# The second block's down projection by pairs of column chunks, with 14 of its 44 block pairs as seven products

## The reference

```python
def conv_ffn(h, w_up, conv_w, conv_b, w_down):
    u = h @ w_up
    u_pad = jnp.pad(u, ((0, 0), (CONV_WIDTH_2 - 1, 0), (0, 0)))
    u = sum(conv_w[j] * u_pad[:, j:j + s] for j in range(CONV_WIDTH_2)) + conv_b
    gate, up = jnp.split(u, 2, axis=-1)
    return (jax.nn.silu(gate) * up) @ w_down
...
        ff = conv_ffn(rms_norm(h, g_ffn_pre[i]), w_up[i], conv_w[i], conv_b[i], w_down[i])
        h = h + rms_norm(ff, g_ffn_post[i])
        e = p[i] @ w_ple_proj[i]
        gate = jax.nn.sigmoid(rms_norm(h, g_ple_in[i]) @ w_ple_gate[i])
        h = h + rms_norm(e * gate, g_ple_post[i])
```

## Time and profile before

| | us |
|---|---|
| median of three runs | 2400.28 (2399.91 to 2403.27) |
| the profiled execution | 2402.21 |
| its span in the trace | 2400.4 |
| PE busy | 2389.7 |
| DVE busy | 1730.3 |
| ACT busy | 1351.6 |
| PE's share of the chain that ended last | 98% |
| granted clock of TensorE, mean | 0.999 |

### The profile page before, as it was taken

How to read it: one execution, slowest core, us unless ns; L and a number is a source line. 1 busy time by engine, 2 the same in 40 slices (tenths; PEclk the granted TensorE clock), 3 DMA queues, 4 the chain that set the end, 5 groups by cost and what they waited for, 6 DMA issues and landing times.

```text
span 2400.4 us, 36297 instructions
## 1 busy us (share of the span) xinstructions
PE 2389.7 (100%) x13245; PEld 2019.9 (84%) x13245; DVE 1730.3 (72%) x2181; ACT 1351.6 (56%) x1729; POOL 47.3 (2%) x105
## 2 busy tenths in 40 slices
PE   9999999999999999999999999999999999999999
PEld 7888888888888888888888888898888888888887
DVE  6578765888888889797578575577777777644475
ACT  5467754555555566456655455466566566444464
POOL 3300000000000000000000000000000000000000
PEclk9999999999999999999999999999999999999999
DMA  8643546566666666656665556566565665666664
GB/s 266 193 143 114 156 160 185 178 206 195 203 188 204 192 198 207 208 190 196 180 186 171 155 154 193 175 201 193 185 196 188 185 194 184 214 194 193 211 197 146
DMA packets 235104, 448.57 MB, mean 187 GB/s; under 512 B 14368, under 2 KB 31604, under 8 KB 234480
## 3 DMA queue, kind: packets, MB, share of 16 engines
q1 hardware_dynamic: 231712, 434.83, 58.0%
q0 software_dynamic: 3280, 12.21, 1.7%
HBM read 443.84 MB, written 3.15 MB: 186 GB/s over the span
## 4 chain that ended last, share of the span: by engine, by line
PE 98%; ACT 1%; DVE 1%; DMA 0%; issue 0%; SPq 0%; ACTq 0%; DVEq 0%
PE pg L2923 12%; PE pg L2925 12%; PE pg L2924 12%; PE pg L3406 7%; PE pg L3408 7%; PE pg L3407 7%; PE pt L3578 7%; PE pg L3578 6%; PE pg L3582 3%; PE pt L3582 3%; PE pg L2982 3%; PE pg L2983 3%; PE pg L2984 3%; PE pt L3408 2%; PE pt L3406 2%; PE pt L3407 2%
## 5 line engine op out<-in xcount | busy, mean ns | idle before, releaser
L1735 DVE TENSOR_TENSOR wlo<-raw,whi 128x1024 fp32r<-128x1024 f32 (+3 forms) x755 | 890.8, 1192 | 545.5 <-ACT whi L826 542.9
L826 ACT ACTIVATE whi<-raw 128x1024 fp32r<-128x1024 f32 (+3 forms) x799 | 819.8, 1034 | 777.4 <-PE pg L2925 412.6
L3578 PE MATMUL pt<-A,whi 128*128 128x512 f32 x704 | 244.8, 391 | 0.0
L3578 PE MATMUL pg<-A,whi 128*128 128x512 f32 x640 | 222.3, 391 | 0.0
L2923 PE MATMUL pg<-whi,A 128*128 128x512 f32 (+1 forms) x576 | 221.5, 385 | 0.0
L2925 PE MATMUL pg<-whi,A 128*128 128x512 f32 (+1 forms) x576 | 218.0, 378 | 0.0
L2924 PE MATMUL pg<-wlo,A 128*128 128x512 f32 (+1 forms) x576 | 217.8, 378 | 0.0
L3582 PE MATMUL pg<-A,wlo 128*128 128x256 f32 x704 | 197.3, 280 | 0.0
L3582 PE MATMUL pt<-A,wlo 128*128 128x256 f32 x704 | 197.1, 280 | 0.0
L3578 PEld LDWEIGHTS pt<-A,whi 128*128 128x128 f32 x704 | 131.7, 187 | 28.9
L3578 PEld LDWEIGHTS pg<-A,whi 128*128 128x128 f32 x640 | 119.7, 187 | 26.2
(11 more groups left out here) (667 smaller groups left out, 4675.9 us busy)
## 6 DMA issues: line engine op xcount, KB each, us to landing
raw<-w_up SPq DMA_DIRECT2D x264, 512.0 KB, 4.4
raw<-w_down SPq DMA_DIRECT2D x176, 512.0 KB, 4.6
raw<-w_in SPq DMA_DIRECT2D x151, 512.0 KB, 3.8
raw<-w_gate SPq DMA_DIRECT2D x88, 512.0 KB, 3.7
raw<-w_out SPq DMA_DIRECT2D x64, 512.0 KB, 3.8
raw<-w_ple_gate SPq DMA_DIRECT2D x32, 512.0 KB, 4.6
raw<-w_in SPq DMA_DIRECT2D x32, 388.0 KB, 3.3
raw<-w_in SPq DMA_DIRECT2D x16, 280.0 KB, 3.0
```

The costliest lines, as they stand in the source:

```text
L826: A(whi[:, n % RING, 0:w], raw[:, n % RING, 0:w], ACT.Copy).then_inc(hi_ready, 1)
L1735: V.tensor_tensor(wlo[:, n % RING, 0:w], raw[:, n % RING, 0:w], whi[:, n % RING, 0:w].bitcast(F32), ALU.subtract).then_inc(lo_ready, 1)
L3578: mm(o.rearrange("p (a n) -> p a n", a=2), wh, A2[:, :, kt, :], start=first, stop=False)
```

## The change

`D_SEVEN` gets a second entry, for the second block: six blocks of the first half (5, 9, 11, 13, 15, 18) and eight of the second (4, 6, 8, 10, 12, 14, 16, 18) are taken as seven products. The loads come in pairs of chunks. The product of the convolution goes to FR in fp32, and FH and FL are made from it in groups of four tiles: group 0 in the second pair of the feed forward loop, the other ten inside the first half of the down projection (`f_hi_part`, `f_lo_part`). ACT does the last pair's convolution ahead of block 6, DVE ahead of block 7. The sums of the activations have only two homes here, so all eight of the second half are made. The results go to FOD by way of sums on DVE; ACT squares them there, and DVE multiplies with the gain (`f_gained`) inside the second half. `last_steps` isn't used in this projection any more. The gain is loaded once the last product of the convolution is there.

```diff
-D_SEVEN = (((3, 6, 8, 12, 14, 18), (3, 6, 8, 10, 12, 14, 16, 18)),)
+D_SEVEN = (((3, 6, 8, 12, 14, 18), (3, 6, 8, 10, 12, 14, 16, 18)), ((5, 9, 11, 13, 15, 18), (4, 6, 8, 10, 12, 14, 16, 18)))
...
-                elif name in ("down1",):
+                elif name in ("down1", "down2"):
...
-                pool.wait_ge(f_lo, 2 * NFF)
+                pool.wait_ge(c_prod, NFF)
                 load(GP[:], a["g_ffn_post_2"][0].partition_broadcast(P), gain_landed)
-                pool.wait_ge(step_used, G["down2"]["N"] + 3 * G["down2"]["S"] + 8)
+                pool.wait_ge(step_used, d_step(1, 1, 7, 0))
...
                 pair(0, 0, between)
-                with act.Fori(0, NFF - 1) as i:
-                    pair(1, i)
+                pair(1, 0, {8: lambda: f_hi_part(1, 0)})
+                with act.Fori(0, NFF - 2) as i:
+                    pair(2, i)
...
-            def f2_hi(c, d):
-                act.wait_ge(c_prod, c + d)
-                A(FH[:, ds((d + c - 1) * 4, 4), :], UC[:], ACT.Copy).then_inc(f_hi, 1)
...
+            def f_squares(p, t, m):
+
+                act.wait_ge(chunk_out[t], DN[1]["C"] + 2 * p + m + 1)
+                act.wait_ge(c_prod, NFF)
+                if p or m:
+                    act.wait_ge(sq_ready, 8 + 4 * p + 2 * m)
+                A(JD[:, t, :], FOD[p][:, t, m * CW:(m + 1) * CW], ACT.Square, accum_out=PS[:, t, 2 * p + m:2 * p + m + 1]).then_inc(sq_ready, 1)
+
+            def down2():
+
+                for p in range(2):
+                    for q in range(2, DQ):
+                        if p == 0 and q == 2:
+                            f2_up(NFF, 0)
+                            d_group(1, 1)
+                        if p == 0 and q == 6:
+                            f2_conv_up(NFF, 0)
+                        if p == 1 and q == 3:
+                            p_parts(1, PHD)
+                        d_blocks(1, p, q)
+                        if p == 0 and q % 2 and q < DQ - 1:
+                            d_group(1, (q + 1) // 2)
+                        if q == D_SEVEN[1][p][-1] + 1:
+                            d_first(1, p)
+                    if p == 0:
+                        for q in range(2):
+                            d_blocks(1, 1, q)
+                            for t in range(NT):
+                                f_squares(0, t, q) if q == 0 else f_squares(0, 1 - t, q)
+                split(DN[1]["end"])
+                split(DN[1]["end"] + 1)
+                root_table()
+                f_squares(1, 0, 0)
+                f_squares(1, 1, 0)
+                f_squares(1, 1, 1)
+                f_squares(1, 0, 1)
...
-                V.tensor_tensor(UC[:], UC[:], GC[:], ALU.mult).then_inc(c_prod, 1)
+                V.tensor_tensor(FR[:, ds((d + c - 1) * 4, 4), :], UC[:], GC[:], ALU.mult).then_inc(c_prod, 1)
...
+                for p in range(2):
+                    y0, y1, y2 = Y0[1][p][:], Y1[1][p][:], Y2[1][p][:]
+                    for q in range(2, DQ - 2):
+                        if p == 0 and q == 2:
+                            f2_up(NFF, 0)
+                            f_lo_part(1, 1)
+                        if p == 0 and q == 7:
+                            f2_conv_up(NFF, 0)
+                        if p == 1 and q == 3:
+                            p_parts(1, PHD, PLD)
+                        if p == 1 and q == 5:
+                            f_gained(0, 0, 0, 1)
+                            f_gained(0, 1, 0, 2)
+                        if p == 1 and q == 7:
+                            f_gained(0, 1, 1, 3)
+                            f_gained(0, 0, 1, 4)
+                        d_blocks(1, p, q)
+                    dve.wait_ge(t_used, d_done(1, p))
+                    add(p, 2, y1, b["P6"], y0)
+                    if p == 0:
+                        d_group(1, DQ // 2 - 1)
...
+                    n = d_step(1, p, DQ, 0)
+                    split(n)
+                    dve.wait_ge(p_run, d_run(1, p, 1))
+                    last(p, 0, 0, b["P2"], y0)
+                    split(n + 1)
+                    dve.wait_ge(step_used, n - 1)
+                    last(p, 1, 0, b["P4"], y2)
+                    if p:
+                        f_gained(1, 0, 0, 1)
+                    else:
+                        split(n + 2)
+                    dve.wait_ge(p_run, d_run(1, p, 2))
+                    last(p, 1, 1, b["X22"], out(1, p, 1))
+                    if p:
+                        f_gained(1, 1, 0, 2)
+                    dve.wait_ge(step_used, n)
+                    last(p, 0, 1, b["P3"], y1)
+                    if p == 0:
+                        split(n + 3)
...
-            down(G["down2"], no, NFF, turn_p)
+            for p in range(2):
+                for q in range(DQ):
+                    if p and q == 2:
+                        pe.wait_ge(u_sum, d_sum(1, 0, 3))
                         p_turn()
+                    d_blocks(1, p, q)
```

More of the change, by code:

```diff
@@ L1618, in _ @@
             if upto < 17: return
-            ffn(F2, [after(f2_up), after(f2_conv_up), lambda c, d: (f2_gate(c, d), after(f2_hi)(c, d)), after(f2_conv_gate)],
+            ffn(F2, [after(f2_up), after(f2_conv_up), f2_gate, after(f2_conv_gate)],
                 {2: f2_in(2), 4: f2_in(3), 6: norm_ffn2, 12: f2_roots, 14: lambda: f2_conv_gate(0, 0)})
[L1622 to L1632, removed]
+            def f_squares(p, t, m):
[4 more added lines that the diff above has]
+                A(JD[:, t, :], FOD[p][:, t, m * CW:(m + 1) * CW], ACT.Square, accum_out=PS[:, t, 2 * p + m:2 * p + m + 1]).then_inc(sq_ready, 1)
@@ L1633, in _ @@
+            down2()
             take_root(7, D)
@@ L1659, in gate_out @@
                 if c == 3 and t == 0:
-                    act.wait_ge(half_used, 3)
+                    act.wait_ge(half_used, 2)
                 else:
@@ L2200, in ffn @@
                 pair(0, 0, between)
-                with dve.Fori(0, NFF - 1) as i:
-                    pair(1, i)
+                pair(1, 0, {9: lambda: f_lo_part(1, 0)})
+                with dve.Fori(0, NFF - 2) as i:
+                    pair(2, i)
             def down(g, hooks, evac, between={}):
@@ L2798, in last_add @@
                 f2_in(2)()
-            ffn(F2, [after(f2_up), after(f2_conv_up), after(lambda c, d: (f2_gate(c, d), f2_lo(c, d))), after(f2_conv_gate)],
+            ffn(F2, [after(f2_up), after(f2_conv_up), after(f2_gate), after(f2_conv_gate)],
                 {1: last_add, 4: f2_in(3), 7: lambda: rstd(6, D), 13: f2_gate_first, 15: lambda: f2_conv_gate(0, 0)})
[L2803 to L2811, removed]
+            def f_gained(p, t, m, n):
+                if p == 0 and n == 1:
+                    dve.wait_ge(gain_landed, 48)
+                dve.wait_ge(sq_ready, 8 + 4 * p + n)
+                x = FOD[p][:, t, m * CW:(m + 1) * CW]
+                ins = V.tensor_tensor(x, x, GP[:, (2 * p + m) * CW:(2 * p + m + 1) * CW], ALU.mult)
+                if n % 2 == 0:
+                    ins.then_inc(gained, 1)
@@ new lines, in down2, with add, last @@
+            def down2():
+                b = d_banks[1]
+                out = lambda t, p, m: FOD[p][:, t, m * CW:(m + 1) * CW]
+                def add(p, i, o, x, y):
+                    dve.wait_ge(u_sum, d_sum(1, p, i - 1))
+                    V.tensor_tensor(o, x, y, ALU.add).then_inc(u_sum, 1)
+                def last(p, t, m, bank, y):
+                    dve.wait_ge(u_sum, d_sum(1, p, 5))
+                    V.tensor_tensor(out(t, p, m), bank, y, ALU.add).then_inc(chunk_out[t], 1)
+                for p in range(2):
[19 more added lines that the diff above has]
+                        d_group(1, DQ // 2 - 1)
+                    split(d_step(1, p, DQ - 2, 0))
+                    add(p, 3, y2, b["P7"], y1)
+                    split(d_step(1, p, DQ - 2, 1))
+                    add(p, 4, y1, b["P5"], y1)
+                    split(d_step(1, p, DQ - 1, 0))
+                    add(p, 5, out(1, p, 1), b["P5"], y2)
+                    split(d_step(1, p, DQ - 1, 1))
+                    n = d_step(1, p, DQ, 0)
[17 more added lines that the diff above has]
+                        split(n + 3)
@@ L2828, in _ @@
             split(g["N"] + 3)
-            post_add(FO, 2)
+            dve.wait_ge(gained, 7)
+            post_add(FOD[1], 2, 2)
             def last_add():
-                evac(3, 0, G["down2"]["end"])
+                f_gained(1, 1, 1, 3)
+                f_gained(1, 0, 1, 4)
                 ple_in(2)()
                 dve.wait_ge(gained, 8)
-                post_add(FO, 3)
+                post_add(FOD[1], 3, 2)
             between = {(0, 1): last_add, (0, 4): ple_in(3), (0, 7): lambda: rstd(8, D)}
@@ L3952, in _ @@
             chunks_read(pe, g["C"] - 1)
-            proj(2, PH, PL)
-            proj(3, PH, PL, lambda: part_0(6, 2))
+            proj(2, PHD, PLD)
+            proj(3, PHD, PLD, lambda: part_0(6, 2))
             pe.wait_ge(h_block, 5)
```

24 lines of the change are left out of this document (9 added, 15 removed).

## The result

The changed kernel takes 2408.22 us (median of 10, 2407.85 to 2410.58); the kernel before took 2401.07 us in 10 runs (2399.83 to 2403.27). The ratio is 1.0030, with a 95% interval of 1.0021 to 1.0038: slower by 7.15 us, where 9.4 was forecast. Fourteen blocks of the second down projection do with 42 matmuls less, and TensorE waits longer than that saves.

What follows compares the result with a forecast made beforehand. PE was taken as the bound, with DVE too slow to feed it: -9.52 + 1.03 + 6.8 + 0.5 + 9.0 + 0.6 + 1.0 = +9.4 us, giving 2409.7 us; own range 2404 to 2415, whole range 2398 to 2420.

Steps and rivals of the forecast that it cites:

- The start: Start of the second block's down projection: PE waits for bank half X22 until DVE's addition ends; +1.03 us.
- How DVE and PE keep step: Down projection: PE waits at a seven-product block if DVE began it under 4.37 us earlier; second-half pairs 11.13 against 10.20.
- Second half: Down projection's second half, blocks 4 to 18: DVE needs 80.3 us, PE 71.4, so PE waits; +9.0 us.
- The lead at block 4: Second half: distance from DVE's start of block 4 to PE's start of it, 4.4 us, nothing to spare.
- First half: Down projection's first half: waits of 0.2 twice, then DVE's pairs 2.12 us short three times; +6.8 us, bounds 4 and 8.
- the gain's load: First half, about T + 37: the moved load may delay the load block 9 waits for; +0.5 us.
- Restarts: Matmuls behind some 12 waits in both halves, recorded with 0.47 instead of 0.39; +1.0 us, bounds 0 and 1.5.
- The end: Behind the last bank: DVE adds before ACT squares, norm 0.9 us later, partly hidden behind proj; +0.6 us.
- DVE keeps up: Rival for the down projection: DVE runs far enough ahead, only start, end and 0.2 of waits remain; 2392.6 us, 17%.
- Only the second half binds: Rival: first half costs only 1.5 us, second 7.5; +1.8, 2402.1 us (2398 to 2405), 19%.
- The clock: Rival: PE falls to 1.2 GHz for ten matmuls behind each of 12 waits; +27 us, 2437, 3%.
- The long DVE: Rival: DVE operations don't overlap, so ten pairs charged at full records cost +10 us; 2419.7 us, 3%.

## Why the prediction was right

- **Removed matmuls, -9.52:** 1014 instead of 1056, by the program; the trace has as many.
- **The start, +1.03:** the matmul at 2055.79 came 1.03 us after its turn, released by DVE's UT, as forecast.
- **How DVE and PE keep step:** the core of the forecast, and right. DVE begins block 5 at T + 20.0 and block 9 at T + 45.4, both as forecast; a pair takes it 11.13 and 12.33 in the second half, 12.33 in the first (12.32 forecast); it has no idle time from block 4 to 18, which take it 80.32 us (80.3 forecast). The first sum of block 9 and the next ones, with splits between, changed kernel:

```profile
2094.45 2.35 DVE L1761 TENSOR_TENSOR wlo<-raw,whi 128x1024 fp32r<-128x1024 f32 x2
2097.39 1.23 DVE L2298 TENSOR_TENSOR DB<-raw 128x1024 f32<-128x1024 f32 x1 [0.58 <-issue]
2108.58 1.22 DVE L1761 TENSOR_TENSOR wlo<-raw,whi 128x1024 fp32r<-128x1024 f32 x1
2109.72 1.22 DVE L2298 TENSOR_TENSOR DB<-raw 128x1024 f32<-128x1024 f32 x1
```

- **Second half, +9.0:** from the turn of p to the projection are 112.82 us. PE's own work in it is 20 blocks of 24 matmuls less 24 for the sevens, 456 x 0.2267, and 0.45 for the turn: 103.8. The rest is 9.0, exactly the forecast, in waits of 2.01, 0.38, 0.80, 0.84, 0.81, 0.81 and 0.83 = 6.5 us and what the slow stretch and the restarts took. The lead at block 4 was 4.48 (4.4 forecast): PE comes to it at T + 145.99, DVE at T + 141.51, and there is no wait. The release takes 0.15, not the 0.08 forecast, so 4.44 was needed and there was indeed nothing to spare.
- **First half, +6.8 with +0.5 for the gain's load:** from T to the turn are 134.64 us; 24 blocks less six times 3 matmuls are 558 x 0.2267 = 126.5, and 1.03 for the start leaves 7.1 for the 7.3 forecast. The load itself cost nothing: block 9 began when it should without it, since the weights that it waited for landed in 4.34 us and only the load before them took longer, 5.26. So that term was 0 and the other 7.1. The two small waits forecast at blocks 7 and 9 are there too, as 0.09 and 0.14 for 0.2 each:

```profile
2090.66 0.50 PE L3493 MATMUL pg<-whi,FH 128*128 128x512 f32 x1
2101.82 0.47 PE L3493 MATMUL pg<-whi,FH 128*128 128x512 f32 x1
```

  They matter because the forecast was to be wrong if the first wait of a half came later than block 9. In the first half it didn't, but by little, as the first long wait is at block 10. The three long waits come at the ordinary blocks 10, 12 and 14, ahead of their first product, and not at 11, 13 and 15. The length of a pair decides the sum, so the place changed nothing, but the text had named the wrong piece.
- **Restarts, +1.0:** the one term that was wrong in kind; the load's and the end's were only too large. The matmul behind a wait is recorded with 0.47, but in a stretch that DVE paces it starts when DVE lets it, whatever the last one took; the 9.0 and 7.1 above hold the restarts already. They had been counted twice.
- **The end, +0.6:** DVE's reduction begins 1.73 us behind the projection's first matmul, where it began 0.92 behind it before. The first matmul of the next stage came 6.81 us behind it (2306.26), against 6.58 before: 0.2, so three quarters of the delay were hidden. The value had been taken too near the upper end.
- **What lies around it:** the down projection's forecast was 8.8 and it took 7.59 more. The rest of the span gave back 1.6 us: T is 2051.99 instead of 2053.10 and the last stretch with the stores is 0.8 shorter, less the 0.2 of the end. T lies between 2051.86 and 2054.50 in the kernels run here, which are alike up to it, so this is within the scatter of single executions and can't be laid to the change.
- **The rivals:** *DVE keeps up* fell, as the windows show DVE busy for 218.34 of 247.49 us and PE released by it. *Only the second half binds* fell with the 12.33 us pairs of the first. *The clock* happened in kind but not in size: two stretches of seven or eight matmuls at 0.43 us instead of twelve of ten, and since another wait followed each, nothing of it was added to the end. The Trainium skill, TensorE: Matmul & The Clock Gate, section "A second HAM failure mode", tells of short idles between groups of matmuls that make the clock swing. The windows above agree with it in kind: the granted clock was 0.51 and 0.52 behind waits of 2.01 us. *The long DVE* fell: at full records a pair would have been over 12.1 us, it was 11.13.

The forecast was +9.4 and +7.15 was measured. The restarts (1.0), the end (0.4), and the load less what the first half took more (0.5 - 0.3) make 1.6 of the difference; the other 0.7 lies around the projection and within what two series differ by. The times themselves, 2409.7 forecast and 2408.22 measured, are only 1.5 apart because the median of before is 0.8 us higher in ten runs than in three. That part of the nearness is luck.

## What to carry to other kernels

Where an engine that feeds the busiest one is at 88% in a stretch, compare the two per unit of work in the order in which it is issued, not in sum: a pair that takes the feeder 11.13 us and the consumer 10.20 costs 0.93 each time, and saves only 0.68. A trick that trades work of the bottleneck for work of its feeder can be laid too densely; here eleven sevens, most with two ordinary blocks between them, in place of fourteen turned +7 us into -5. In such a stretch any work moved off the feeder's chain, even a half us of waiting caused by order, came out of that stretch one for one (2.45 us for 2.4, 5.65 for 5.7), unless it went to an engine that contends with the feeder.

## What the runs showed of the hardware

- **The clock behind waits.** Behind PE waits of 1.98 to 2.20 us, 20 in seven profiled executions, nine were followed by a stretch of seven or eight matmuls at 0.43 us pitch (granted clock near 0.5, 1.2 GHz), which cost 1.4 us; behind the waits of 0.4 to 1.7 us, some sixty in all profiled executions, none was (both kinds counted in the second block's down projection). The same program showed it behind different waits in two executions.
- **GpSimd beside DVE.** When both add from SBUF, they take turns: a DVE split of 1.22 us was recorded with up to 2.32 and ended 1.09 us behind GpSimd's addition; over the second half this line (wlo for a seven's first chunk) averaged 1.83 us against 1.22. GpSimd's addition of 512 columns took 1.3 us at best and up to 3.9 with its waits, DVE's 0.69.
- **A megabyte beside the weights.** Four loads of 512 KB took a median of 6.6 us to land behind GpSimd's load of 1 MB, and 4.2 at the same place without it.
